# Differential attention on one core: VectorE combines the two softmax halves before it takes the next tile's maximum

## The reference

```python
s = jnp.einsum('bqhcd,bkhcd->cbhqk', qi, k).astype(jnp.float32) * scale
p = jax.nn.softmax(s, axis=-1)
a = (p[0] - lam * p[1]).astype(v.dtype)
return jnp.einsum('bhqk,bkhv->bqhv', a, v)
...
o = rms_norm(o, subln) * (1.0 - lam_init)
return gated_out(o.reshape(b, n, D_INNER), g, w_out)
```

## Time and profile before

| | us |
|---|---|
| median of 3 runs | 2520.59 |
| profiled execution, its own time | 2512.74 |
| its span, first to last instruction | 2511.0 |
| PE busy | 2259.2 (90%) |
| DVE busy | 1116.8 (44%) |
| ACT busy | 790.4 (31%) |
| POOL busy | 316.0 (13%) |
| granted TensorE clock, mean share of full | 0.949 |

### The profile page before, as it was taken

How to read it: one execution, slowest core, us unless ns; L and a number is a source line. 1 busy time by engine, 2 the same in 40 slices (tenths; PEclk the granted TensorE clock), 3 DMA queues, 4 the chain that set the end, 5 groups by cost and what they waited for, 6 DMA issues and landing times. The chain is left out here.

```text
span 2511.0 us, 34283 instructions
## 1 busy us (share of the span) xinstructions
PE 2259.2 (90%) x13793; PEld 2152.7 (86%) x13793; DVE 1116.8 (44%) x1457; ACT 790.4 (31%) x1327; POOL 316.0 (13%) x104
## 2 busy tenths in 40 slices
PE   6799889979996999999899999789888888887996
PEld 1799857979995999999899999778788878887995
DVE  2745195463115323232110111187778887774112
ACT  2421143122113000000121212266566766664111
POOL 0200000000102323232100000031122221100100
PEclk9899799889997999999999999899999999998997
DMA  7545244384213232333232322322113321107224
GB/s 281 202 164 164 88 165 144 108 300 177 86 58 154 76 102 80 102 86 102 76 113 75 111 81 81 137 81 99 35 65 99 99 84 36 64 15 266 79 91 170
DMA packets 89040, 288.48 MB, mean 115 GB/s; under 512 B 9584, under 2 KB 36336, under 8 KB 81520
## 3 DMA queue, kind: packets, MB, share of 16 engines
q1 hardware_dynamic: 87792, 282.39, 32.7%
q10 hardware_dynamic: 1152, 4.72, 0.5%
HBM read 204.72 MB, written 82.31 MB: 114 GB/s over the span
## 5 line engine op out<-in xcount | busy, mean ns | idle before, releaser
L410 PE MATMUL p_ps<-p_h_hi,p_w_hi 128*128 128x384 f32 x1536 | 351.5, 336 | 33.8 <-DVE p_h_lo L492 33.8
L410 PE MATMUL p_ps<-p_h_hi,p_w_lo 128*128 128x384 f32 x1536 | 350.2, 335 | 0.0
L410 PE MATMUL p_ps<-p_h_lo,p_w_hi 128*128 128x384 f32 x1536 | 350.1, 335 | 0.0
L410 PEld LDWEIGHTS p_ps<-p_h_hi,p_w_hi 128*128 128x128 f32 x1536 | 275.4, 189 | 37.0 <-issue 28.2
L410 PEld LDWEIGHTS p_ps<-p_h_lo,p_w_hi 128*128 128x128 f32 x1536 | 275.1, 189 | 0.0
L410 PEld LDWEIGHTS p_ps<-p_h_hi,p_w_lo 128*128 128x128 f32 x1536 | 275.0, 189 | 0.0
L481 DVE TENSOR_TENSOR p_w_lo<-p_w_raw,p_w_hi 128x2048 fp32r<-128x2048 f32 x40 | 96.3, 2409 | 282.4 <-ACT p_w_hi L436 282.4
L1230 PE MATMUL o_ps<-o_y_hi,o_w_hi 128*128 128x384 f32 x768 | 176.7, 337 | 33.1 <-DVE o_w_lo L1284 31.0
L547 DVE SCALAR_TENSOR_TENSOR p_xs<-p_ps,p_cs 128x1152 f32<-128x1152 f32 x64 | 83.9, 1353 | 274.0 <-PE p_ps L410 274.0
L436 ACT CAST p_w_hi<-p_w_raw 128x2048 fp32r<-128x2048 f32 x40 | 76.3, 1908 | 362.1 <-PE p_ps L410 361.9
L1559 PE MATMUL a_ps<-a_v_hi,a_at_hi 128*128 128x256 f32 x584 | 181.9, 311 | 7.5 <-DVE a_g L1778 5.1
(11 more groups left out here) (232 smaller groups left out, 4043.0 us busy)
## 6 DMA issues: line engine op xcount, KB each, us to landing
p_w_raw<-w_in_dram SPq DMA_DIRECT2D x40, 1024.0 KB, 6.2
g_dram<-p_stage SPq DMA_DIRECT2D x32, 576.0 KB, 3.0
f_w_raw<-w_u_dram SPq DMA_DIRECT2D x32, 512.0 KB, 3.7
o_w_raw<-w_out_dram SPq DMA_DIRECT2D x32, 512.0 KB, 4.3
f_g<-g_dram SPq DMA_DIRECT2D x8, 1152.0 KB, 7.8
y_dram<-f_y SPq DMA_DIRECT2D x8, 1152.0 KB, 5.3
x_dram<-o_x_new SPq DMA_DIRECT2D x16, 576.0 KB, 5.1
q_dram<-p_stage SPq DMA_DIRECT2D x32, 288.0 KB, 3.3
```

The costliest lines, as they stand in the source:

```text
L410: mm = pe.matmul(ps[:, 4 * b + c, 0:CH], a, x[:, c * CH:(c + 1) * CH], start=(d == 0 and j == 0), stop=(d == DT - 1 and j == 2))
```

## The change

The last three operations of DVE's step change places. Before, the order was `maximum(ahead, 0)`, `low_half(back, 2)`, `combine(now)`. Now it is `combine(now)`, `low_half(back, 2)`, `maximum(ahead, 0)`. No operation is added or removed, and no other engine's program changes.

```diff
@@ -1788,9 +1788,9 @@
                 gate(back2)
                 weigh(now)
                 low_half(back, 1)
+                combine(now)
+                low_half(back, 2)
                 maximum(ahead, 0)
-                low_half(back, 2)
-                combine(now)
```

## The result

The changed kernel takes 2565.6 us (median of 4 runs, 2562.67 to 2567.81) against 2520.5 us of the kernel before (4 runs, 2519.76 to 2521.04). The ratio is 1.0179, with a 95% interval of 1.0164 to 1.0194: 45 us or 1.8% slower. The forecast was 2551 us, with a range of 2535 to 2569. The direction, the mechanism of the loop and the outer range held. The size was 15 us short, and the forecast's own narrower range, 2543 to 2560, was missed. One later run of the kernel before, 2652.8 us at a granted clock of 0.82 where the others have 0.95, is left out of all comparisons.

A forecast was written before the change was run, and what follows sets the result against it. Bounds taken: PE's work with ACT's chain close behind in quiet steps, the held combination in POOL's steps. Stage 573.3 + 64.5 + 6.2 = 644.0 against 615.4, plus 1.6 at the start: +30.2, 2551 us; range 2535 to 2569.

The forecast's parts named there:

- The removal: On DVE the combination starts 0.6 us before POOL's subtraction; 81 us of holding and PE's 54.1 us of waiting should go.
- The loop: Chain of starts through DVE and ACT, now in single file: every full step costs 9.29 us, with POOL or without.
- the 0.20 us term: The small low part on DVE, `low_half(back, 2)`, counted in each full step between combination and maximum: 0.20 us.
- Rival A: The held combination was the real limit and the chain through ACT hides: faster, 2466 us; chance 0.05.
- rival B: Gain and loss cancel, which needs a full step of 8.7 us: 2516 to 2525 us; chance 0.04.
- `ofac` under POOL: DVE's one-column `ofac` is held by POOL's v subtraction once in each of seven heads: 1.8 us each.
- rival C: `ofac` is not held by POOL, as nothing shows that a single column is: 2538 us; chance 0.15.
- rival D's first stage: PE's clock still falls once a head, 13 us in all: 2564 us; chance 0.14 for this or oftener.
- the likeliest case: The forecast itself, with PE's clock left alone: 2551 us, own range 2543 to 2560; chance 0.62.
- The start: First combination stands ahead of a maximum, so the stage's first `ofac` comes about 1.6 us later.
- The two turns of the loop: PE spends some 3.06 us on instructions at each of two turns; kept as 2 x 3.1 = 6.2 us.
- The steps of the short tile: In each head, two steps holding the short tile as `now` or `back`: 8.5 us each, estimated between 7.79 and 9.29.

The follow-up runs named there:

- first experiment: The changed kernel with `ofac` made by a tensor_scalar (one tensor input) instead of a tensor_tensor: 2550.7 us, ratio 1.0124 to the kernel before.

## Why the prediction was right, and where it was short

**The removal.** The combination first by 0.6 us: right, it is 0.5 to 0.6. POOL's rows are longer for their wait, PE's 54.1 us are 2.9. The runs with POOL's reads taken out give the worth of it, 60 us, of which the rival that counted PE's waits alone had 54.

**The loop.** 9.29 us forecast, 9.27 measured, in steps with POOL and without. It was not only consistent with the rows: taking out the 0.20 us term shortened every full step by 0.19, and taking the exponential out of the chain shortened it by 0.69. Rival A (the chain hides) and rival B (the two cancel) fell by the step alone, at 9.27 against the 7.8 and 8.7 that they needed.

**`ofac` under POOL.** Taken at the upper bound of 1.8 us, against a rival C of nothing. Measured 1.67 us in seven instances, 1.5 more than usual. The row of line 481 was the right guide, though it has 2048 columns and `ofac` one. The Trainium skill (SBUF — State Buffer, Who interferes with whom) states the rule for a DVE instruction with two SBUF inputs beside a GpSimd one that reads SBUF. The runs agree with it in three parts. The instruction that comes second is held until the first ends (`ofac`, 1.67 and 1.99 us). A DVE instruction with one SBUF input is free (0.21 us); the Trainium skill says so for instructions outside DVE's 2-port modes, and no run shows in which mode this one ran. A GpSimd instruction that only writes holds nothing (1.41 us).

**The step that failed** is the sentence "I assume that the shorter gaps of the changed step, under 2 us each, leave the clock alone." It failed twice. In the v step PE's gap is not under 2 us but 2.61: PE has only the short tile's scores to do there and waits 1.15 us in any case (first experiment), and the hold on `ofac` comes on top. I had priced that hold on DVE and not carried it on to PE. The clock went to 0.50 for a part or all of the rest of the step, which is 10.59 us in the mean against 9.17, 7 x 1.42 = 10 us. And gaps under 2 us do not always leave the clock alone. At a head's second tile PE waits 1.88 to 1.95 us for the exponential; in three heads of seven the clock falls behind it and the step takes 9.73 us instead of 9.27:

```profile
1811.10 0.81 PE L1522 MATMUL a_ps<-a_k_hi,a_q_hi 128*128 128x384 f32 x3 [1.88 <-ACT a_e L1628]
```

```profile
1812.00:1822.00 10.00, 6.53 (x40) 5.82 (x38) 6.43 (x11) 6.49 (x14) 3.41 (x1) 0.83 0.06 13
```

The mean of 0.83 is a mixture of 0.50 and 1.00. The row that the assumption leaned on, 0.99 from 1893 to 1930, could not bear it. PE's longest gap in that stretch is 0.84 us:

```profile
1893.25 0.66 PE L1537 MATMUL a_ps<-ident,a_e 128*128 128x128 f32 x4 [0.84 <-DVE a_e L1757]
```

The first experiment shows that the gap of 2.61 is not even needed, as the short tile's step loses 1.3 us in most heads without it. Which gaps bring the clock down, and which do not, stays open: the same gap does both.

Of the two open prices, rival D's first stage (once a head, 13 us) was the right one, and the likeliest case should have had it in: its time was 2564 and the median is 2565.6. That it came so near is in part luck, for the clock cost 10 us there and not 13, and the terms below made up the rest.

**The smaller terms.** The start cost 5.0 and not 1.6: the first combination stands under POOL's first v subtraction in both kernels, and took 2.45 us with a maximum ahead of it, and takes 3.82 us without:

```profile
1633.84 2.45 DVE L1757 SCALAR_TENSOR_TENSOR a_e<-a_e,a_ratio 128x1152 f32<-128x1152 f32 x1
```

```profile
1638.73 3.82 DVE L1757 SCALAR_TENSOR_TENSOR a_e<-a_e,a_ratio 128x1152 f32<-128x1152 f32 x1
...
1643.86 1.22 ACT L1628 ACTIVATE a_e<-a_ps,a_nmax 128x1152 f32<-128x1152 f32 x1 [5.67 <-DVE a_nmax L1723]
```

The instruction moved forward waits longer for the same event, and with the maximum behind it instead of ahead the exponential waits 5.67 us, where it waited 1.81. The two turns of the loop cost 7.7 us rather than 6.2 over the usual step. The steps of the short tile came to 17.0 against 17.0, but the 8.5 was the middle between two bounds and not worked out, so that is luck. The last head took 66.3 us instead of 64.5: its last two steps were put at about 10.7 and took 12.5. They took 12.1 already in the kernel before, so that estimate missed a row that was there. 10 for the v step, 1.5 for the turns, 1.4 for the three steps of 9.73 and 1.8 for the last head, less some 50 x 0.02 for the loop, are the 13.8 us between 644.0 and 657.8. The sum had no term for what lies behind the last `ofac`, where 1.7 us go.

## What to carry to other kernels

An instruction that looks expensive because it is held should be asked what it covers: here the held combination was also the work beside another engine's chain, and moving it out of the collision took away the cover. Before moving it, write the loop of starts through all engines with the term left out, and compare it with the present step. If two engines collide on a port, look first at who can wait for free (POOL, a head ahead of its need) and at whether the instruction needs two tensor inputs at all. When a hold is found, follow it to the matrix engine and price the clock behind the gap. A row shows a safe gap only up to the longest gap in it.

## What the runs showed of the hardware

A DVE tensor_tensor of one column per partition is held like a large one by a POOL subtraction: 4921 ns was the longest, in the kernel where POOL waits for the combination:

```profile
L1768 DVE TENSOR_TENSOR a_ofac<-a_orstd,a_linv x72: 158/160/4921, 1648.1 to 2294.4; 128x1 f32<-128x1 f32 x72
```

The same product as a tensor_scalar with a per-partition scalar costs 0.05 us more and is not held in any of its 72 instances. A full maximum over PSUM (at most 1.36 us), the low parts of 512 columns (one input in PSUM, at most 0.69) and the gate (at most 0.43) kept their usual times beside POOL. In these traces a hold on either engine shows as a longer instruction, not as idle time: POOL's q subtraction reads 3.45 us where it works 2.67.
